# A two-layer transformer block on one core: who modulates the norms, how far apart the delta net's hops stand, and a pipeline's last step moved into the next head

## The reference, cut to what matters

```python
def _rmsnorm(x, g):
    y = x32 * lax.rsqrt(jnp.mean(x32 * x32, axis=-1, keepdims=True) + RMS_EPS)
    ...
def _modulate(h, shift, scale):
    return h * (1.0 + scale) + shift
```

```python
    sol = lax.linalg.triangular_solve(a_strict + jnp.eye(C, dtype=F32), rhs, left_side=True,
                                      lower=True, unit_diagonal=True)
    u, w = sol[..., :dv], sol[..., dv:]
    ...
    def step(S, inp):
        v_new = u_i - jnp.einsum('bhcd,bhde->bhce', w_i, S)
        o = (jnp.einsum('bhcd,bhde->bhce', q_i * jnp.exp(g_i)[..., None], S)
             + jnp.einsum('bhij,bhje->bhie', a_i, v_new))
        S = (S * jnp.exp(g_last)[..., None, None]
             + jnp.einsum('bhcd,bhce->bhde', k_i * jnp.exp(g_last[..., None] - g_i)[..., None], v_new))
```

## Time and profile before

| what | value |
|---|---|
| median of 3 runs | 2575.03 us (2574.2 to 2575.14) |
| the profiled execution | 2575.85 us |
| its span, first to last instruction | 2574.0 us |
| mean granted TensorE clock | 0.987 |
| busy share | PE 96%, DVE 40%, ACT 29%, POOL 21% |

### The profile page before, as it was taken

The page is one execution under the profiler, slowest core; times in us unless marked ns, Lnnn a source line. Parts: engine busy times, 40 slices in busy tenths (PEclk is TensorE's granted clock), DMA queues, the critical chain, the costliest instruction groups (busy, mean ns, idle before and its releaser), DMA issues. The chain is left out here.

```text
span 2574.0 us, 40331 instructions
## 1 busy us (share of the span) xinstructions
PE 2479.8 (96%) x15613; PEld 1573.6 (61%) x15614; DVE 1023.8 (40%) x2361; ACT 735.3 (29%) x1603; POOL 543.7 (21%) x501
## 2 busy tenths in 40 slices
PE   7999999989999999999899999999999999999998
PEld 4565565555555555555676677766645449468484
DVE  2454455427667675113454454544442111010110
ACT  3454445221222220103354444544331111110110
POOL 0211111023323233331443234432100000000000
PEclk9999999989999999998999999999999999999999
DMA  8234222313333333211111010110339998685931
GB/s 263 72 83 131 74 72 74 108 49 98 110 117 98 115 113 95 57 45 57 35 35 34 18 35 18 35 34 11 98 106 321 345 346 270 209 274 161 291 111 29
DMA packets 323361, 299.02 MB, mean 116 GB/s; under 512 B 5952, under 2 KB 285632, under 8 KB 323104
## 3 DMA queue, kind: packets, MB, share of 16 engines
q1 hardware_dynamic: 318880, 281.58, 35.9%
q0 software_dynamic: 4352, 15.60, 2.5%
HBM read 281.95 MB, written 13.63 MB: 115 GB/s over the span
## 5 line engine op out<-in xcount | busy, mean ns | idle before, releaser
L1381 PE MATMUL bank<-hidden,weight_ring 128*128 128x384 f32 x704 | 238.7, 493 | 4.9 <-ACT hidden L451 4.9
L687 PE MATMUL bank<-weight_ring,hidden 128*128 128x384 f32 x672 | 236.8, 496 | 1.6 <-ACT work L861 1.3
L1530 DVE SCALAR_TENSOR_TENSOR weight_ring<-weight_ring,silu_c 128x256 f32<-128x256 f32 x308 | 213.7, 735 | 5.5
L1381 PEld LDWEIGHTS bank<-hidden,weight_ring 128*128 128x128 f32 x704 | 133.2, 192 | 93.7 <-issue 7.0
L1381 PE MATMUL bank<-weight_ring 128*128 128x384 f32 x528 | 181.1, 493 | 0.3 <-DVE work L1538 0.3
L687 PEld LDWEIGHTS bank<-weight_ring,hidden 128*128 128x128 f32 x672 | 121.5, 191 | 92.0 <-issue 15.4
L2653 PE MATMUL bank<-work 64*64 64x64 f32 x4608 | 156.9, 220 | 8.6 <-DVE weight_ring L3427 6.5
L2653 PEld LDWEIGHTS bank<-work 64*64 64x64 f32 x4608 | 145.9, 135 | 16.4 <-POOL work L3123 5.5
L1914 PE MATMUL bank<-work,weight_ring 128*128 128x224 f32 x768 | 147.7, 354 | 0.0
L1914 PEld LDWEIGHTS bank<-work,weight_ring 128*128 128x128 f32 x768 | 144.1, 190 | 1.9 <-ACT work L1989 1.6
L1381 PEld LDWEIGHTS bank<-weight_ring 128*128 128x128 f32 x528 | 99.4, 191 | 69.9 <-issue 5.9
(11 more groups left out here) (445 smaller groups left out, 4030.0 us busy)
## 6 DMA issues: line engine op xcount, KB each, us to landing
weight_ring<-in_moe_w_in SPq DMA_DIRECT2D x64, 1024.0 KB, 10.3
weight_ring<-in_ada_w SPq DMA_DIRECT2D x38, 1024.0 KB, 5.2
weight_ring<-in_ffn_w_in SPq DMA_DIRECT2D x44, 512.0 KB, 4.9
hidden<-in_moe_w_out SPq DMA_DIRECT2D x8, 2816.0 KB, 11.7
residual<-in_moe_w_out SPq DMA_DIRECT2D x8, 2816.0 KB, 16.5
work<-in_moe_w_in SPq DMA_DIRECT2D x16, 1024.0 KB, 10.7
weight_ring<-in_na_w_qkv SPq DMA_DIRECT2D x24, 512.0 KB, 9.9
weight_ring<-in_gdn_w_qkv SPq DMA_DIRECT2D x24, 512.0 KB, 4.4
```

Source lines behind the costliest of these rows:

```text
L687: mm = nc.tensor.matmul(m.psum[6][:, 0:3 * P], m.H[:, k, t * P:(t + 1) * P], weights(u)[:, k, :], start=(k == 0), stop=(k == KD - 1))
L1381: mm = nc.tensor.matmul(bank[:, 0:HT], w[:, k, :], t[:, k, :], start=(first and k == 0), stop=(last and k == HK - 1), skip_group_check=True)
L1530: nc.vector.scalar_tensor_tensor(out=out, in0=ada_slab[:, k, :], scalar=by, in1=out, op0=ALU.mult, op1=ALU.add).then_inc(acc_ok, 1)
```

## The change

**Norms.** ACT modulates the 8 latent pieces, and a new list on POOL, on_pool, the 8 context pieces (128x256) with one tensor_scalar each (multiply, add, both factors from a column). Where code waited for ready(k), it now waits for both. In swiglu POOL does this behind the first four sums of weight blocks; in delta_net it does it ahead of the first four.

```diff
+    def on_pool(self, pool):
...
+        for k in range(KD):
+            pool.wait_ge(scaled, self.base[4] + k * len(self.parts) + 2)
+            nc.gpsimd.tensor_scalar(self.hidden(k, 1), self.hidden(k, 1), m.MODA[:, self.layer, self.norm, k, v:v + 1],
+                                    m.MOD[:, self.layer, 3 * self.norm, k, v:v + 1], ALU.mult, ALU.add).then_inc(context, 1)
...
             body(0, 0)
+            pre.on_pool(pool)
             pool.wait_ge(tokens_ok, 1)
...
+            pre.on_pool(pool)
             weight_sums(0, lambda name: GP.credit - SUMS - 3 if name == "s4" else 1, *KV)
```

**Router.** 8 matmuls in the place of 14:

```diff
-            for _ in range(14):
+            for _ in range(8):
                 nc.tensor.matmul(B[2][:, 0:HALF], ident, const(m, C_CUMF, HALF), start=True, stop=True)
```

**Hops.** On PE the hops of steps 8 to 11 stand two products of the inverse apart where it was one, and the list ends with the last kv ahead of the two u products:

```diff
                 first(0, 0)
+                first(0, 1)
                 tx(8)
-                first(0, 1)
+                second(0, 0)
+                second(0, 1)
                 kv(8)
-                second(0, 0)
+                third(0, 0)
+                third(0, 1)
                 ks(9)
...
+                    first(GROUPS, d)
+                kv(11)
                 for d in range(2):
                     pe.wait_ge(act_step, SC.after(h, f"Y{GROUPS}.{d}"))
                     pe.wait_ge(dve_step, VE.after(h, f"Xc{GROUPS - 1}.{d}"))
                     multiply(1 + d, Y, U, d, f"u.{d}")
-                turn_out()
```

**The output chain.** turn_out goes from the end of body h to the next body, behind the first three matmuls of P1 (in the last body, which prepares nothing, to the very front), and out_o with it. On ACT square_o and root_o go behind the last take_y, and on DVE sum_o, arg_o and inv_o go behind UF1:

```diff
                 block_product("P1", 0, 3)
+                turn_out(h - 1)
                 tx(0)
...
                 if not prep:
+                    turn_out(h - 1)
                     for s in range(STEPS):
...
                 take_b(1, 0)
-                sum_o()
                 take_b(1, 1)
+                st(10)
                 take_c(1, 0)
-                arg_o()
+                x(11)
                 take_c(1, 1)
-                inv_o()
...
                     less(UF, 1 + d, d, f"UF{d}")
-                out_o()
+                sum_o()
+                arg_o()
+                inv_o()
```

More of the change, by code:

```diff
@@ L255, in load_and_norm @@
     m.first_sems = slab_in, ada_product, ada_copied, ada_summed, mod_sum, mod_scale, const_in
-    m.norm_sems = semaphores(m, "norm", "summed root inverted spread scaled hidden")
-    _, root, inverted, spread, scaled, _ = m.norm_sems
+    m.norm_sems = semaphores(m, "norm", "summed root inverted spread scaled hidden context")
+    _, root, inverted, spread, scaled = m.norm_sems[0:5]
     parts = [(CTX, TOK, 0), (0, CTX, 1)]
-    m.norm_base = [0, 1, 1, 2, 3 * KD, KD]
+    m.norm_base = [0, 1, 1, 2, 3 * KD, KD, 0]
     m.parts = parts
@@ L2599, in gate_part, with turn_out @@
                         mm.then_inc(pe_scan_step, TS.step("gate"))
-                def turn_out():
-                    if not scan:
+                def turn_out(scanned):
+                    if scanned < 1:
                         return
-                    pe.wait_ge(act_scan_step, SS.before(h, "gate"))
-                    pe.wait_ge(pool_scan_step, GS.before(h, "on"))
+                    pe.wait_ge(act_scan_step, SS.before(scanned, "gate"))
+                    pe.wait_ge(pool_scan_step, GS.before(scanned, "on"))
                     for t in range(4):
@@ L2868, in body @@
                 first(0, 0)
+                first(0, 1)
                 tx(8)
-                first(0, 1)
+                second(0, 0)
+                second(0, 1)
                 kv(8)
-                second(0, 0)
+                third(0, 0)
+                third(0, 1)
                 ks(9)
-                second(0, 1)
+                fourth(0, 0)
                 tx(9)
-                third(0, 0)
+                fourth(0, 1)
                 kv(9)
-                third(0, 1)
+                first(1, 0)
+                first(1, 1)
                 ks(10)
-                fourth(0, 0)
+                second(1, 0)
+                second(1, 1)
                 tx(10)
-                fourth(0, 1)
+                third(1, 0)
+                third(1, 1)
                 kv(10)
-                first(1, 0)
+                fourth(1, 0)
                 ks(11)
-                first(1, 1)
+                fourth(1, 1)
                 tx(11)
-                second(1, 0)
-                kv(11)
-                second(1, 1)
-                for d in range(2):
-                    third(1, d)
-                for d in range(2):
-                    fourth(1, d)
                 for d in range(2):
                     first(GROUPS, d)
+                kv(11)
                 for d in range(2):
@@ L3094, in body @@
                 take_y(0, 0)
+                take_y(0, 1)
                 vn(8)
-                take_y(0, 1)
                 oa(9)
                 vn(9)
+                take_y(1, 0)
+                take_y(1, 1)
                 oa(10)
                 vn(10)
-                take_y(1, 0)
                 oa(11)
-                take_y(1, 1)
                 vn(11)
+                for d in range(2):
+                    take_y(GROUPS, d)
                 square_o()
                 root_o()
-                for d in range(2):
-                    take_y(GROUPS, d)
             turns(act, body)
@@ L3323, in inv_o, with out_o @@
                         nc.vector.reciprocal(rstd_o, rstd_o).then_inc(dve_scan_step, VS.step("inv_o"))
-                def out_o():
-                    if not scan:
+                def out_o(scanned):
+                    if scanned < 1:
                         return
-                    dve.wait_ge(pe_scan_step, TS.before(h, "ot"))
-                    turned, gates, to = (a.rearrange("p (t s n) -> p t s n", t=4, s=2) for a in (B[GATE][:, :], gate, m.O[:, h - 1, :]))
+                    dve.wait_ge(pe_scan_step, TS.before(scanned, "ot"))
+                    turned, gates, to = (a.rearrange("p (t s n) -> p t s n", t=4, s=2) for a in (B[GATE][:, :], gate, m.O[:, scanned - 1, :]))
                     for half in range(2):
@@ L3340, in body @@
                 if not prep:
+                    out_o(h - 1)
                     dve.wait_ge(kept, 32)
@@ L3355, in body @@
                     add_group(6)
-                    out_o()
+                    out_o(h)
                     add_group(7)
                     return
+                out_o(h - 1)
                 st(0)
```

105 lines of the change are left out of this document (53 added, 52 removed).

## The result

The changed kernel took 2599.3 us (median of 4 runs, 2597.11 to 2600.26), the kernel before 2574.61 in the same series. The ratio is 1.0095, with a 95% interval of 1.0083 to 1.0108: slower by 25 us. The forecast was 2598.5.

The account below looks back on a forecast made before the run. PE was taken to bound the kernel, busy 2479.8 of 2574.0 us. Terms -10.2 - 1.8 + 26.5 + 9 + 0.3 + 1.0 - 1.3 = +23.5 on 2575.03 gave 2598.5 us, range 2586 to 2606.

Parts of the forecast that it names:

- The output chain: At turn_out, PE waits for POOL's scaling, 3.5 us six times and 5.5 in the last body: +26.5 us.
- E: The moment the last u product of a head's inverse is done; UF1 can't start sooner; POOL's scaling forecast at E + 5.6.
- The clock: Behind five or six of the seven turn_out pauses, PE runs 3 us at half speed: +9 us.
- The hops, -10.2, and x(6), -1.8: Delta net heads: hops two products apart shorten the inverse, 1.45 us a head; x(6) moved up on DVE, 0.25 a head.
- The FFN's norm: Context pieces on POOL, taken at 0.58 us each, in the FFN's norm: +0.3 us (-0.5 to +1.3).
- The delta net's norm: POOL's weight sums beside DVE's differences block each other, z's copy comes late and PE follows: +1.0 us (0 to +1.7).
- The router: Sixteen throwaway matmuls in place of 28 ahead of the router's gathered work: -1.3 us (0 to -1.3).
- the chain was not hidden: Rival: the output chain stays hidden, only the gains and small terms stand, -12.0 us, 2563; chance 0.05.
- the clock did not stay: Rival: the stall at turn_out comes but PE's clock stays, +14.5 us, 2589.5; chance 0.13.
- the hops gained: Denies the rival that hops gain nothing, losses only moving to other hops: +33.7 to +35.5, 2609 to 2610; chance 0.05.
- not over 4: Denies the rival that distance between hops gains over 4 us a head: -28 against +35, some 2582; chance 0.05.
- The rival of the upper ends: Rival: low clock follows every pause, losses at their upper ends: +36, with half the excesses about +30, 2605; chance 0.10.

Follow-up runs that it names:

- e1_chain_only: The kernel before with only the output chain moved; hops, norms and router as before: 2616.66 us, ratio 1.0163.
- e4_covered: The changed kernel with sum_o ahead of UF0, and turn_out and tx(0) behind all of P1 and half of P2: 2564.01 us, 0.9957 of before.
- e6_turn_at_end: The changed kernel with turn_out and out_o back at the end of the same body and sum_o ahead of UF0: 2596.73 us, 1.0082 of before.
- e2_stall_filled: The changed kernel with 8 unread matmuls (13 in the last body) filling PE's wait ahead of turn_out: 2584.36 us, 1.0036 of before.
- e11: e8 with x(6) put back behind left(q) on DVE, as before: 2563.11 us, 0.9953 of the kernel before.
- e3: The kernel before with only both norms' context pieces moved to POOL: 2576.02 us, ratio 1.0005.
- e8: e4_covered with the first four output projection units ahead of turn_out in the last body: 2559.76 us, 0.9942 of the kernel before.
- e5: The changed kernel with one edit, DVE's sum_o ahead of UF0 and not behind UF1: 2576.25 us, 1.0003 of the kernel before.
- e9: The kernel of e8 run once more, unchanged: 2558.55 us, 0.9938 of the kernel before.

## Why the prediction was right, point by point

- **The output chain, +26.5.** Measured 26.4, seven pauses of 3.46 (six) and 5.6, by the mechanism stated: sum_o at E + 0.6, POOL done at E + 5.5, six matmuls of P1 ahead of turn_out. e1_chain_only shows it without the rest of the change, e4_covered takes it away. One thing was not foreseen: the hops' distance would have cost 3.7 us a head here by itself (e6_turn_at_end), since it puts the last oa 1.6 us before the end of the inverse. The loss comes from where the chain was put, not from its being moved.
- **The clock, +9.** The mechanism was right and the size too small: 13.8 by the landmarks and 14.9 by the medians (e2_stall_filled). All seven pauses were followed by 0.50, where five or six were expected, and two of the stretches were twice as long as the 3 us on which the term rested. The 2 us a pause are a mean: against 80.57 (80.64 less 0.07 for the longer filling) the periods are 1.7 to 1.9 us longer in five heads and 3.1 in one.
- **The hops, -10.2, and x(6), -1.8.** The inverse went from 24.05 to 22.05, so 2.0 a head and -14 in place of -10.2, above the upper bound of 1.8. The waits that were read (0.52 and 0.36) are gone; so is a third one that was not read, 0.21 for POOL's L3190 ahead of a product (seven times before, not once now). What is left, 2.0 - 1.23 - 0.21, is 0.6, where the changes between products and hops were taken for 0.2; that it is their price is not shown by itself. x(6) gave 0.44 a head in place of 0.25 (e11). Together they are 2.34 a head in e2_stall_filled, or 16.4 us, where 1.7 and 12 were forecast.
- **The FFN's norm, +0.3.** 1.0 in the changed kernel's trace, within the bounds; +0.1 to +2.2 over all nine. The value for the piece, 0.58, was good: 0.56 and 0.55. What the term left out is the overlap: one of the eight pieces took 2.08 beside a difference on DVE, the same blocking that the forecast counted for the delta net. The Trainium skill's rule (GPSIMD Engine Reference, section 4.1) had the piece near the copy's 0.40. The measured 0.56 lies halfway to the two-tensor operation's 0.68, and no run has the same operation on VectorE, so the rule itself stays untested.
- **The delta net's norm, +1.0.** -1.3 in the changed kernel's trace, -0.3 where the clock is alike (e3 above). The step that failed is "PE follows through it": T4 ended 2.7 us later behind the norm's start (3.5 and more was stated), z's copy came 0.4 sooner there, and in the late traces, where it comes 0.3 to 0.8 later than before, PE's landmark is no later. The other 1 us is the low clock at P1 and P2, which ended 3 us sooner; the forecast did not look at it, and that it helped here is luck.
- **The router, -1.3.** -2.6. The bound of 1.3 rested on SP's next transfer as the moment of landing; by the other traces the gain is 1.2 to 2.9.

The terms as measured in the traces (the -1.3 with its 1 us of clock) sum to -16.4 + 26.4 + 13.8 + 1.0 - 1.3 - 2.6 = +20.9, beside 21.2 in the spans of the two profiled executions and 24.7 in the medians. The profiled execution of the changed kernel was the fastest of its four. The total was hit because errors of both signs, up to 5 us each, cancelled, which is luck; the stall, the largest term, was right by its mechanism. Four rivals fall by a run: the chain was not hidden (e1), the clock did not stay (e2), the hops gained (e2, e4), and they gained 2.3 to 2.5 a head, not over 4. The rival of the upper ends was half right: every pause was followed by the low clock, at more than its 11.5, while the hops gave more and not less.

## What to carry to other kernels

When a step is moved across a loop's end, measure its chain from the first instruction that it now stands behind, on each engine, and compare that with the work that is ahead of its consumer in the consumer's own list; here 5.5 against 2.0. Three matmuls more ahead of turn_out, with sum_o ahead of UF0 and UF1, turned 25 us lost into 11 gained (e4), and four units of work ahead of the last turn_out made it 15 (e8). A pause of a few microseconds on a busy TensorE costs more than its length: here 3.5 us cost 5.5 on average, and 1.6 us no more than itself. A hop or product whose row is longer than its likes' holds a wait that no list of waits shows; compare the durations of the same instruction along its list, at the same granted clock, before deciding what a reordering can win. And before a landmark's shift is put down to the change, compare the granted clock in it: here 1.0 of 1.3 us was the clock.

## What the runs showed of the hardware that was not expected

- The low clock behind a pause of the same length lasts differently, and once it didn't come: behind six pauses of 3.46 us in the changed kernel it lasted 3.4 us five times and 6.8 once, in e1_chain_only it stayed away behind one of six, and behind the last body's pause of 3.72 us in e5 it lasted 10.2 us, the first 1.8 of them inside the pause. Six pauses of 1.59 us (e5) were followed by none, one of 2.2 us (e4) by 3.4 us. In e11 3.4 us at 0.50 came in the last body behind 9.5 us in which PE was never idle for more than 0.54 us at a time; its tail is 1.4 to 2.3 us longer than those of e8 and e9.
- DVE's differences of 128x1536 and POOL's sums of 128x512, both on two inputs in SBUF, take turns: 1.75 becomes 2.7 to 2.8 for all but the first and 1.28 becomes 2.7 to 2.8, nearly the sum of both (3.03) for each. That agrees with the Trainium skill, page SBUF — State Buffer, section SBUF: two separate sides, by which such a pair of operations holds a shared port in turn, each for its whole length. A piece with one tensor input on POOL took 2.08 beside such a difference in place of 0.55.
- Filling a pause with products that nobody reads made the kernel 14.9 us faster at the same length of pause.
